# Two-layer hybrid backbone on one core: late vectors of layer 1, outputs by direction, four rounded buffers for w2, six for the dense units, decays ahead of modulation rows, ranks in four column groups

## The chip, the core and the metric

The kernel runs on one core of a Trainium2 chip. A core has five engines, each with an instruction stream of its own: TensorE (PE, with PEld for its weight loads), VectorE (DVE), ScalarE (ACT), GpSimd (POOL) and SyncE (SP), which here only issues DMAs. They meet at semaphores. The metric is the device time of one execution in microseconds (us); lower is better.

## What is computed

512 token columns (256 of context, 256 latent) go through two layers: a mixer (gated linear attention with two directions beside a short convolution), then a feed-forward part, dense in layer 0 and top-2 of 8 experts in layer 1. All is float32. The reference, cut to its skeleton:

```python
for i in range(2):                       # x: latent, xc: context, same weights
    p = split_proj(modulate(rmsnorm(x, g_mix_pre[i]), sh1, sc1) @ w_in[i])   # q k v g a_f a_b B C h
    la_f = log_sigmoid(a_f @ w_dec[0] + b_dec[0]) / 16     # a_f, a_b: 16 ranks each
    la_b = log_sigmoid(a_b @ w_dec[1] + b_dec[1]) / 16
    o = scan_forward(q, k, v, la_f) + scan_backward(q, k, v, la_b)   # chunks of 64
    y = concat(rmsnorm(o) * silu(g), B * conv3(C * h)) @ w_out[i]
    x = x + gt1 * rmsnorm(y)
    h2 = modulate(rmsnorm(x, g_ffn_pre[i]), sh2, sc2)
    x = x + gt2 * rmsnorm((silu(h2 @ w1) * (h2 @ w3)) @ w2 if i == 0 else experts(h2))
```

The shifts, scales and gates (sh1, sc1, gt1, ...) are rows of `silu(c) @ w_mod[i] + b_mod[i]`, for the latent and for the context stream.

## The kernel before

Everything is kept transposed: features on 128 partitions, the 512 tokens along the free axis, so that `x` is eight tiles of 128x512 (k = 0 to 7). Every engine has its program in one fixed order, written by hand; `plan()` fixes the order of the PSUM tiles and their banks, and with it the order in which SP loads the weights: chunks of 2 MB into four slots of `ring`, each loaded when the last reader of the slot's earlier chunk has finished. The experts then use the whole ring as 12 slots of 1 MB.

**Split products.** Projections and the dense feed-forward multiply fp32r words in three products (`product`, L755 to L757): high x high, high x low and low x high. High words are roundings. DVE makes the weights' (`split_in`, `split_unit`, `split_step`: a CAST L1683 and a subtraction L1686, of 128x1024 words for a unit). ACT makes the high words of x with the modulation (`modulate`, L1376), then the full words (L1379), and DVE subtracts for the low words (`low_row`, L1686 on `hT_rounded`). The rounded weights rotate through three buffers in the projections (`in_w_high`), three in the dense units (`w_high`) and two in the w2 steps (`w2_high`, with `ff_high` and `ff_low`).

**Start.** SP loads x and four modulation chunks. PE transposes x (L771), makes modulation rows (`mod_rows`, L719: eight fp32 products of 32 columns, in four column groups of the array), transposes them back (`mod_cols`, L727) and sums squares (L688). DVE scales x (`normalise`, L1745) and then takes all four modulation columns (`take_mods`, L1803 to L1815). ACT issues 11 small DMAs for the vectors of layer 1 (`load_vectors(1)`, the last of them w_decay, L1330), PE transposes them (`vectors(1)`, L763), and ACT takes the result before it modulates (`take_vectors(1)`, L1393).

**Mixer.** PE: q and k over the rows k; the ranks `a` as a split product with 32 output columns; DVE masks them into two copies (L1839, L1840); four products `z` with w_decay (L814) on 32 rows; v; seven rounds of scores (`scores`, L845) between the projections g, C, h and B, for whose masks DVE builds decays (`differences`, L1934) and takes the scores (L1890); modulation rows ("keys"); transposed keys `kt` (L870); chunk products `U` (L885); DVE's chain of states for both directions (L1981, L1983), and then PE's outputs `o` (L901, and L913 with the states). The convolutions `conv(0)` to `conv(3)` (L1898 to L1918) are DVE's, and conv(3) stands ahead of the decays for the states (L1944, ACT's exponential L1479, L1949). ACT copies the modulation rows (`take_rows`, L1409) ahead of those exponentials.

**Feed-forward.** Layer 0: 44 units of 24 products (gate and up), three of them started row by row; then w2 in 2 x 22 steps of 12 products. Layer 1: experts of 65 to 128 tokens take the split path `mid` (L1163 to L1170), those under 65 the path `few` (L1093, L1119), which streams 42 MB in plain fp32.

## Time and profile before

| what | value |
|---|---|
| median of 3 runs | 1905.54 us (1905.01 to 1905.95) |
| profiled execution: its time / its span | 1906.78 / 1905.0 us |
| PE busy / DVE busy / ACT busy | 89% / 49% / 28% |
| DMA queue of the weights | 474 MB, mean 250 GB/s over the span |

The span is the time from the first to the last instruction; 1.78 us of the execution lie around it. The first 945 us are the mixers and the dense part, the other 960 the experts. In a timeline row the idle time of the engine ahead of an instruction stands in brackets, with what ended it.

### The profile page before, as it was taken

The numbers are of one execution on the slowest core, as the hardware profiler recorded it, in microseconds if no ns is written. First come the engines' busy times: TensorE is split into PE (matmuls) and PEld (weight loads), VectorE is DVE, ScalarE is ACT, GpSimd is POOL, SyncE is SP. The second block draws the span as 40 slices with busy tenths as digits, with TensorE's granted clock in tenths as the row PEclk, the third lists the DMA queues.
The fourth block names the chain that finished last, engine by engine and source line by source line (L and its number), as shares of the span: only waits on it lengthen the run. The fifth ranks groups of instructions, "written<-read, shape, count | busy, mean of one in ns | idle before, by whom it ended". The sixth has DMA issues, their size and how long they took to land.

```text
span 1905.0 us, 20538 instructions
## 1 busy us (share of the span) xinstructions
PE 1700.9 (89%) x8358; PEld 1151.1 (60%) x8358; DVE 941.1 (49%) x1291; ACT 536.5 (28%) x682; POOL 5.0 (0%) x14
## 2 busy tenths in 40 slices
PE   5899899999999998989899799887877999787877
PEld 2688665888887775877688688433236873322322
DVE  3388665544436666693588688301017871010102
ACT  2521134300000015323477477100005750000001
POOL 0000000000000000000000000000000000000000
PEclk8899999999999998999799999998998999989998
DMA  9210775233221244333799699699999988999996
GB/s 358 91 57 32 261 270 186 80 116 105 88 78 45 78 172 152 118 139 131 269 375 374 220 374 376 252 394 394 394 394 381 382 325 313 396 391 394 394 394 257
DMA packets 223832, 476.26 MB, mean 250 GB/s; under 512 B 9906, under 2 KB 32724, under 8 KB 223700
## 3 DMA queue, kind: packets, MB, share of 16 engines
q1 hardware_dynamic: 222176, 474.24, 68.1%
q8 instruction: 88, 1.44, 0.3%
q10 hardware_dynamic: 1524, 0.21, 0.1%
q14 instruction: 44, 0.36, 0.1%
HBM read 473.38 MB, written 1.05 MB: 249 GB/s over the span
## 4 chain that ended last, share of the span: by engine, by line
PE 72%; DMA 11%; DVE 5%; SPq 5%; issue 4%; ACT 2%; ACTq 1%; DVEq 0%; POOL 0%; POOLq 0%
PE ps L755 11%; PE ps L756 11%; PE ps L757 11%; DMA ring<-in_e_w 10%; PE ps L1093 7%; PE ps L1163 6%; PE ps L1165 6%; PE ps L1170 6%; SPq L629 3%; PE ps L1119 2%; PE ps L688 2%; SPq L633 2%; PE ps L719 2%; PE ps L951 1%; PE ps L1050 1%
## 5 line engine op out<-in xcount | busy, mean ns | idle before, releaser
L1093 PE MATMUL ps<-ring,work 128*64 128x512 f32 x1120 | 278.3, 645 | 80.6 <-DMA ring<-in_e_w 60.7
L1093 PEld LDWEIGHTS ps<-ring,work 128*64 128x64 f32 x1120 | 90.5, 148 | 247.9 <-issue 247.9
L2158 DVE TENSOR_TENSOR mixT<-work,ps 64x256 f32<-64x256 f32 x70 | 29.7, 424 | 417.3 <-ACT work L1567 416.2
L1686 DVE TENSOR_TENSOR ring_rounded<-ring,hT_rounded 128x2048 fp32r<-128x2048 f32 x84 | 191.7, 2288 | 27.8 <-ACT hT_rounded L1586 20.5
L755 PE MATMUL ps<-ring_rounded 128*128 128x512 f32 (+2 forms) x464 | 171.5, 370 | 7.1 <-DVE hT_rounded L1686 5.2
L1586 ACT CAST hT_rounded<-ring 128x2048 fp32r<-128x2048 f32 x84 | 159.9, 1911 | 46.4 <-PE ps L1165 36.2
L757 PE MATMUL ps<-ring_rounded 128*128 128x512 f32 (+2 forms) x400 | 142.3, 356 | 0.0
L755 PE MATMUL ps<-mixT_rounded,work_rounded 128*128 128x512 f32 x352 | 137.7, 391 | 2.9 <-DVE hT_rounded L1686 2.1
L757 PE MATMUL ps<-mixT_rounded,ring_rounded 128*128 128x512 f32 x352 | 137.4, 390 | 0.0
L756 PE MATMUL ps<-hT_rounded,work_rounded 128*128 128x512 f32 x352 | 137.4, 390 | 0.0
L1119 PE MATMUL ps<-ring,mixT 128*64 128x512 f32 x560 | 125.8, 593 | 0.0
L1163 PE MATMUL ps<-hT_rounded,work_rounded 128*128 128x512 f32 x252 | 103.4, 410 | 21.7 <-issue 18.5
L756 PE MATMUL ps<-hT_rounded,ring_rounded 128*128 128x512 f32 (+2 forms) x336 | 117.8, 351 | 0.0
L1683 DVE CAST work_rounded<-ring 128x1024 fp32r<-128x1024 f32 (+1 forms) x88 | 49.1, 558 | 121.7 <-PE ps L757 121.7
L1686 DVE TENSOR_TENSOR ring_rounded<-ring,norms_rounded 128x2048 fp32r<-128x2048 f32 x42 | 96.1, 2289 | 23.1 <-ACT norms_rounded L1586 23.1
L755 PEld LDWEIGHTS ps<-ring_rounded 128*128 128x128 f32 (+1 forms) x464 | 89.1, 192 | 27.4 <-issue 10.0
L1165 PE MATMUL ps<-hT_rounded,work_rounded 128*128 128x512 f32 x252 | 101.2, 401 | 0.0
L1170 PE MATMUL ps<-ring_rounded,work_rounded 128*128 128x512 f32 x336 | 91.8, 396 | 0.0
L1119 PEld LDWEIGHTS ps<-ring,mixT 128*64 128x64 f32 x560 | 41.6, 137 | 76.1 <-issue 70.0
L1569 ACT COPY mixT<-ps 128x256 f32<-128x256 f32 x35 | 13.0, 373 | 256.7 <-PE ps L1107 256.7
L1686 DVE TENSOR_TENSOR ring_rounded<-ring,work_rounded 128x1024 fp32r<-128x1024 f32 (+1 forms) x88 | 84.1, 955 | 1.5
L757 PEld LDWEIGHTS ps<-ring_rounded 128*128 128x128 f32 (+1 forms) x400 | 75.9, 190 | 11.7
(247 smaller groups left out, 2663.5 us busy)
## 6 DMA issues: line engine op xcount, KB each, us to landing
ring<-in_e_w SPq DMA_DIRECT2D x336, 1024.0 KB, 14.1
ring<-in_w_mod SPq DMA_DIRECT2D x24, 2048.0 KB, 9.6
ring<-in_w_in SPq DMA_DIRECT2D x12, 2048.0 KB, 7.9
ring<-in_w SPq DMA_DIRECT2D x22, 1024.0 KB, 7.9
ring<-in_w_out SPq DMA_DIRECT2D x4, 2048.0 KB, 13.7
ring<-in_w SPq DMA_DIRECT2D x4, 2048.0 KB, 7.9
ring<-in_w SPq DMA_DIRECT2D x2, 1536.0 KB, 9.2
mixT<-in_ctx SPq DMA_DIRECT2D x2, 512.0 KB, 4.3
```

The source lines that it names most:

```text
L629: sp.dma_start(dst.rearrange("p (k n) -> p k n", k=4), rows(w[0, e, k0 * P:(k0 + 4) * P], b * BLK, BLK)).then_inc(piece_in[s], 16)
L755: pe.matmul(acc, w_high_, x_high_, start=first, stop=False)
L756: pe.matmul(acc, w_high_, x_low_, start=False, stop=False)
L757: return pe.matmul(acc, w_low_, x_high_, start=False, stop=last)
L1093: ins = pe.matmul(acc[H * w:H * w + H, :], x[:, k, 0:H], piece_words(e, b, 2 * half + w)[:, kk * BLK:(kk + 1) * BLK], start=(k == 0), stop ...
L1119: ins = pe.matmul(ps[0][H * half:H * half + H, :], eh[:, b % 2, ((j % 2) * 2 + j // 2) * H:][:, 0:H], piece_words(e, b, 4 + i)[:, o:o + BL ...
L1163: pe.matmul(outs[q], high[q], w_high_[:, cols], start=q < first, stop=False, skip_group_check=True)
L1165: ins = pe.matmul(outs[q], low[q], w_high_[:, cols], start=False, stop=False, skip_group_check=True)
L1170: ins = pe.matmul(outs[q], high[q], w_low_[:, q * BLK:(q + 1) * BLK], start=False, stop=q >= 4 - last, skip_group_check=True)
L1586: act.copy(highs[at_ % HIGHS], piece_words(e, b, i)).then_inc(high_ready, 1)
L1683: return dve.tensor_copy(dst, src)
L1686: return dve.tensor_tensor(dst, src, high, ALU.subtract)
```

## The change

- `vectors(1)` and its loads come after layer 0's `z`; w_decay has a semaphore of its own and is loaded four times, once for each group of 32 partitions. ACT issues these 18 small DMAs behind layer 0's modulation.
- The start: DVE takes modulation columns 0 and 1 ahead of the scaling, columns 2 and 3 after three of its eight rows, and scales the others between the splits. `modulate` waits for each half of the scale alone.
- `row_products`: in the row-by-row stages (q/k, first three dense units) PE does both products with x's high words on all tiles, then the products with the low words.
- `a` is no longer a split unit: 16 plain fp32 products in four column groups, and `z` sums over all 128 partitions.
- conv(3) comes after the "keys" modulation columns, and ACT takes these rows after the exponentials of the decays.
- Outputs by direction: `states_ready` counts directions. Layer 0 does its heads in two pairs; layer 1 does all four heads with direction 0, then the modulation rows `states1`, then direction 1.
- Six rounded buffers for the dense units, four for w2's row tiles; the first two w2 steps are split ahead of the last unit's product. The split of `qk` 3 of layer 1 stands inside `normalise`.

```diff
-    IN_UNITS += [("qk", L_, p) for p in range(PAIRS)] + [("a", L_, 0)] + [("v", L_, p) for p in range(PAIRS)]
+    IN_UNITS += [("qk", L_, p) for p in range(PAIRS)] + [("v", L_, p) for p in range(PAIRS)]
...
+        w2_parts = [part(at_, 3, 512, of=of) for of, at_ in ((ring_r, HIGH_AT), (ring_r, HIGH_AT + 1536), (work_r, 0),
+                                                             (work_r, 1536))]
+        def unit_high(u):
+            return in_w_high[:, u - 3].rearrange("p (k n) -> p k n", k=KD) if 3 <= u < 6 else w_high[:, u % 3]
...
+            def row_products(n, tiles, x_high_, x_low_, first, last):
+                pe.wait_ge(high_row, n + 1)
+                for acc, c0, w_high_, w_low_ in tiles:
+                    pe.matmul(acc, w_high_, x_high_[:, c0:], start=first, stop=False)
+                    pe.matmul(acc, w_low_, x_high_[:, c0:], start=False, stop=False)
+                pe.wait_ge(x_split, n + 1)
+                for acc, c0, w_high_, w_low_ in tiles:
+                    ins = pe.matmul(acc, w_high_, x_low_[:, c0:], start=False, stop=last)
...
             mod_cols(*start[-1])
-            vectors(1)
...
-                project_in(("a", L), ("a", L, 0), 0, width=2 * RANK)
+                for x_ in (in_high, x_low):
+                    for kk in range(2):
+                        for g in range(4):
+                            k = 4 * kk + g
+                            ins = pe.matmul(acc[2 * RANK * g:2 * RANK * (g + 1), :], w[:, k, 0:2 * RANK],
+                                            x_[:, k, :].bitcast(F32), start=(kk == 0 and x_ is in_high),
+                                            stop=(kk == 1 and x_ is x_low), skip_group_check=True)
...
+                if L == 0:
+                    vectors(1)
...
-                mods("states1" if L else "states")
+                if L == 0:
+                    mods("states")
...
+                for pairs in ((0,), (1,)) if L == 0 else ((0, 1),):
...
+                    for d in range(2):
+                        if L and d == 1:
+                            mods("states1")
+                        pe.wait_ge(states_ready, 2 * L + d + 1)
+                        pe.wait_ge(state_ops, 4 * L + 3 + d)
...
-                wait_mods(layer, s + 1)
+                    if k in (0, 4):
+                        act.wait_ge(mod_ready, 12 * layer + 2 * s + 3 + k // 4)
...
-            load_vectors(1)
-            take_vectors(1)
...
                 modulate(2 * L, L, 0, 0, in_high)
+                if L == 0:
+                    for layer in range(DEPTH):
+                        load_decay(layer)
+                    load_vectors(1)
...
-                take_rows(*MODS["keys1" if L else "keys"])
-
                 for d in range(2):
                     act.wait_ge(state_diff, 2 * L + d + 1)
...
+                take_rows(*MODS["keys1" if L else "keys"])
...
-                if k == 0:
-                    wait_tile(dve, unit_tile(UNITS - 1) if half == 0 else ("y2", 3))
+                if d in (2, 3):
+                    wait_tile(dve, unit_tile(UNITS - 1))
...
-            normalise(0, 0)
-            take_mods(*MODS["start"])
+            take_mods(*MODS["start"][0:2])
+            r = inverse(TOK)
+            for k in range(3):
+                divide(hT[:, k, :], xT[:, k, :], r)
+            take_mods(*MODS["start"][2:4])
...
-                conv(3)
...
                 take_mods(*MODS["keys1" if L else "keys"])
+                conv(3)
...
+                        if j == JF - 1:
+                            split_step(0)
+                            split_step(1)
```

What now stands where, on the engines that wait there. DVE at the start, from the scaling of x (`hT<-xT,norms`) to the first low word of x (`hT_rounded`); before:

```order
L1679 COPY xT<-ps 128x512 x8
L1745 TENSOR_TENSOR hT<-xT,norms 128x512 x8
L1803 TENSOR_REDUCE modv<-ps 128x8
L1807 TENSOR_TENSOR modv<-modv,vecs 128x8
...
L1683 CAST ring_rounded<-ring 128x1024
L1686 TENSOR_TENSOR ring_rounded<-ring,ring_rounded 128x1024
L1686 TENSOR_TENSOR hT_rounded<-hT,ring_rounded 128x512 x2
```

The same stretch now:

```order
L1738 COPY xT<-ps 128x512 x8
L1863 TENSOR_REDUCE modv<-ps 128x8
L1867 TENSOR_TENSOR modv<-modv,vecs 128x8
L1863 TENSOR_REDUCE modv<-ps 128x8
L1867 TENSOR_TENSOR modv<-modv,vecs 128x8
L1803 TENSOR_TENSOR hT<-xT,norms 128x512 x3
...
L1742 CAST ring_rounded<-ring 128x1024
L1745 TENSOR_TENSOR ring_rounded<-ring,ring_rounded 128x1024
L1745 TENSOR_TENSOR hT_rounded<-hT,ring_rounded 128x512
L1803 TENSOR_TENSOR hT<-xT,norms 128x512
```

Two modulation columns moved ahead of the scaling, and five of its eight rows behind the first split. PE from the ranks to v (`work,ring` is z, `ident,work` the vectors); before and now:

```order
L755 MATMUL ps<-ring_rounded 32x512
L756 MATMUL ps<-hT_rounded,ring_rounded 32x512
L757 MATMUL ps<-ring_rounded 32x512
L814 MATMUL ps<-work,ring 128x512 x4
L755 MATMUL ps<-ring_rounded 128x512
```

```order
L842 MATMUL ps<-ring_rounded,ring 32x512 x8
L842 MATMUL ps<-hT_rounded,ring 32x512 x8
L851 MATMUL ps<-work,ring 128x512 x4
L793 MATMUL ps<-ident,work 128x113
L770 MATMUL ps<-ring_rounded 128x512
```

Eight such triples became 16 plain products, and the vectors stand behind z. DVE at the end of layer 0's scores, from the last taken level but one; before and now:

```order
L1890 COPY_PREDICATED work<-masks,ps 128x512 x4
L1898 TENSOR_TENSOR norms<-norms,ps 128x512
...
L1918 TENSOR_TENSOR mixT<-mixT,ps 128x512
L1944 TENSOR_TENSOR work<-work 128x1024 x2
L1949 TENSOR_TENSOR work<-work 128x1024 x2
```

```order
L1955 COPY_PREDICATED work<-masks,ps 128x512 x4
L2008 TENSOR_TENSOR work<-work 128x1024 x2
L2013 TENSOR_TENSOR work<-work 128x1024 x2
L1955 COPY_PREDICATED work<-masks,ps 128x512 x4
L2017 TENSOR_TENSOR work<-work 128x1024 x2
```

The six instructions of conv(3) left the stretch ahead of the decays.

## Rows read from the trace of the kernel before

**Rows 1.** Waits of PE: by whom, total, times, longest.
```profile
PE ps L1093 <- DMA ring<-in_e_w: 60.7, 25, 3.5
```
**Rows 2.** Waits of SP's DMA queue for a slot.
```profile
SPq L629 <- PE ps L1170: 252.1, 84, 21.9
```
**Rows 3.** Timeline, the start.
```profile
31.82 1.92 PE L719 MATMUL ps<-ring,csil 128*32 128x512 f32 x16 [0.55 <-DMA ring<-in_w_mod]
32.80 4.91 DVE L1745 TENSOR_TENSOR hT<-xT,norms 128x512 f32<-128x512 f32 x8 [14.49 <-ACT norms L1361]
37.86 1.11 PE L727 MATMUL ps<-ident,ring 128*128 128x128 f32 x4 [4.11 <-DVE modv L1803]
47.84 0.45 PE L763 MATMUL ps<-ident,work 113*128 113x113 f32 x1 [6.96 <-DMA ring<-in_w_decay]
51.41 0.76 PE L755 MATMUL ps<-ring_rounded 128*128 128x512 f32 x1 [3.13 <-DVE hT_rounded L1686]
```
**Rows 4.** DMA issues of 18.9 to 19.3 (q/k) and 243.3 to 243.6 (w_out): KB, us to landing.
```profile
ring<-in_w_in SPq DMA_DIRECT2D x1, 2048.0 KB, 18.9
ring<-in_w_out SPq DMA_DIRECT2D x1, 2048.0 KB, 13.4
```
**Rows 5.** Stretches: length, PE busy (instructions), PEclk, DMA share, GB/s.
```profile
81.30:113.40 32.10, 30.61 (x107) 0.84 0.23 85
82.80:89.10 6.30, 6.30 (x9) 0.57 0.93 338
352.25:575.50 223.25, 223.25 (x984) 1.00 0.29 92
732.20:739.00 6.80, 6.00 (x20) 0.50 0.68 260
758.50:788.90 30.40, 28.91 (x107) 0.89 0.25 90
```
**Rows 6.** Timeline, z in layers 0 and 1.
```profile
82.79 6.33 PE L814 MATMUL ps<-work,ring 32*128 32x512 f32 x8 [1.49 <-DVE work L1840]
760.04 4.35 PE L814 MATMUL ps<-work,ring 32*128 32x512 f32 x8 [1.49 <-DVE work L1840]
```
**Rows 7.** Timeline, layer 0 from the scores to y.
```profile
224.67 3.65 PE L870 MATMUL ps<-ident,work 128*128 128x128 f32 x16 [3.37 <-DVE work L1890]
246.15 2.02 PE L901 MATMUL ps<-work 128*128 128x128 f32 x16 [0.77 <-DVE small L1992]
256.78 0.69 DVE L1683 CAST ring_rounded<-ring 128x1024 fp32r<-128x1024 f32 x1 [5.83 <-DMA ring<-in_w_out]
257.51 1.23 DVE L1686 TENSOR_TENSOR ring_rounded<-ring,ring_rounded 128x1024 fp32r<-128x1024 f32 x1
269.28 0.50 PE L755 MATMUL ps<-ring_rounded 128*128 128x512 f32 x1 [0.78 <-DVE norms L2008]
```
**Rows 8.** Timeline, dense part and entry of layer 1.
```profile
330.55 1.09 ACT L1376 ACTIVATE mixT_rounded<-hT,modv 128x256 fp32r<-128x256 f32 x2
352.25 0.47 PE L755 MATMUL ps<-mixT_rounded,work_rounded 128*128 128x512 f32 x1 [0.85 <-DVE ring_rounded L1686]
578.28 0.47 PE L755 MATMUL ps<-work_rounded 128*128 128x512 f32 x1 [2.75 <-DVE ring_rounded L1686]
642.14 0.47 PE L755 MATMUL ps<-work_rounded 128*128 128x512 f32 x1 [2.15 <-DVE ring_rounded L1686]
733.00 0.55 PE L755 MATMUL ps<-ring_rounded 128*128 128x256 f32 x1 [2.07 <-DVE hT_rounded L1686]
```
**Rows 9.** Timeline, layer 1 from the scores to y.
```profile
854.11 2.76 PE L870 MATMUL ps<-ident,work 128*128 128x128 f32 x16 [2.63 <-DVE work L1949]
859.36 3.81 DVE L1983 SCALAR_TENSOR_TENSOR hT<-hT,dec,ps 128x128 f32<-128x128 f32 x12
865.22 3.57 PE L719 MATMUL ps<-ring,csil 128*32 128x512 f32 x16 [3.03 <-DVE hT L1983]
878.95 1.32 PE L951 MATMUL ps<-mixT,ring 128*128 128x256 f32 x5 [0.56 <-issue]
```

More of the change, by code:

```diff
@@ L376, in hybrid_backbone @@
         iota_t = work[:, 1408:1408 + TOK].bitcast(I32)
[L377 removed]
+        iota_r = work[:, 1920:1921].bitcast(I32)
         itmp = work[:, 2048:2048 + P]
@@ L748, in project_in @@
                 for k in range(KD):
-                    ins = product(acc[0:width, 0:TOK - c0], high[:, k, :], low[:, k, :], in_high[:, k, c0:],
+                    ins = product(acc[:, 0:TOK - c0], high[:, k, :], low[:, k, :], in_high[:, k, c0:],
                                   x_low[:, k, c0:], k == 0, k == KD - 1)
@@ L799, in _ @@
                         high, low = in_unit(("qk", L, k // 2))
[L800 to L806 removed]
+                    tiles = [(accs[i][:, 0:TOK - job[3]], job[3], high[:, k % 2, i * P:(i + 1) * P],
+                              low[:, k % 2, i * P:(i + 1) * P]) for i, job in enumerate(jobs)]
+                    ins = row_products(2 * L * KD + k, tiles, in_high[:, k, :], x_low[:, k, :], k == 0, k == KD - 1)
                     if k % 2 and k < KD - 1:
                         ins.then_inc(pair_used, 1)
[L809 removed]
+                acc = begin(("a", L))
+                w = weights(("a", L))
+                for x_ in (in_high, x_low):
[5 more added lines that the diff above has]
+                                            stop=(kk == 1 and x_ is x_low), skip_group_check=True)
+                end(ins)
                 wait_drained(pe, ("a", L))
+                pe.wait_ge(wdec_in, 16 * 4 * DEPTH)
                 for i in range(4):
@@ L971, in _ @@
                         pe.wait_ge(w_split, u + 1)
-                        high, low = w_high[:, u % 3], unit_weights(u, ring_r)
+                        high, low = unit_high(u), unit_weights(u, ring_r)
                         for k in range(KD):
@@ L1676, in _ @@
             dve.tensor_copy(itmp, ident[:]).then_inc(consts_done, 1)
+            band = rank_rows[:, 1:2]
+            step(dve.tensor_scalar(band, iota_r, -0.5, None, ALU.is_gt))
+            for edge in range(RANK, P, RANK):
+                wait_step()
+                step(dve.scalar_tensor_tensor(out=band, in0=iota_r, scalar=edge - 0.5, in1=band, op0=ALU.is_gt,
+                                              op1=ALU.subtract))
+            wait_step()
+            step(dve.tensor_scalar(rank_rows[:, 0:1], band, -1.0, None, ALU.mult))
+            step(dve.tensor_scalar(band, band, 1.0, None, ALU.add))
             for k in range(KD):
@@ L1751, in inverse, with normalise @@
                 return rs[:, (n_rs[0] - 1) % 2, 0:n]
-            def normalise(norm, c0, split=None):
+            def normalise(norm, c0, split=None, between=()):
                 r = inverse(TOK - c0)
@@ L1759, in normalise @@
                         low_row(norm, k - 2, *split)
+                    if k == 5:
+                        split_in(*between)
                 if split:
@@ L2039, in _ @@
                                ("ffu", j))
-                    for d in range(2 * JF):
+                    for d in range(2, 2 * JF):
                         split_step(d)
+                    wait_step_used(dve, 2 * JF - 3)
                     split_in(("qk", 1, 0), ("qk", 1, 1), ("qk", 1, 2))
```

134 lines of the change are left out of this document (67 added, 67 removed).

## The prediction

> **What bounds the kernel now.** First the page, for whether there is one bound: PE is busy 89% of the span (the table above), yet it isn't the bound everywhere. PE's waits, by whom, show the difference: in the sparse experts (L1093) it waits 60.7 us for expert weights [rows 1], and there the DMA stream sets the pace. SP's own waits show the reverse for the split experts: its queue waits 252.1 us, 84 times, for PE's L1170 to give a slot back [rows 2]. Two of the three split experts come first (945 to 1217 us). So the stream is ahead of PE when the sparse ones begin, and an earlier start of the experts moves everything behind it by as much. What is left are the first 945 us. All edits lie there, and I read them as a timeline, gap by gap: at each I ask who ends PE's wait, and who would end it next. The instants below are those of the trace of before.
>
> **The start.** Three things in a row hold PE until 51.41 [rows 3]: DVE's scaling (from 32.80, 4.91 us) stands ahead of the modulation columns, so PE waits 4.11 us until 37.86; then the vectors of layer 1 cost a DMA round trip (6.96 us of idle before 47.84); then comes the first low row. What doesn't move is the DMA queue: the fourth modulation chunk ends PE's wait at 31.82 [rows 3], and q/k's chunk, issued at 19.01, lands 18.9 us later, at 37.9 [rows 4]. Afterwards: modulation rows until 33.8, columns and copy with 0.8 us between them until 36.4; ACT modulates from 35.3. DVE can split q/k's first unit only at 37.9: 0.69 + 1.23 us [rows 7], with the handover 2.0, so PE starts at **40.0**. From there PE wants 12 products of 0.227 us a row (223.25 us for 984 products [rows 5]), 2.7 us; ACT needs 1.97 (four instructions; a pair takes 1.09 [rows 8]), DVE 2.3 (half a split, a scaling of 0.62, a low row of 0.69). PE stays the bound. Gain 11.4. The clock is low when PE starts, as before; I put the same loss in both, and 1.5 us either way in the range. The 18 DMA issues on ACT take some 0.32 us each, 5.8 us behind the last modulated row, until 58.3; q's drain behind them is due at 64, w_decay at 67, so they are hidden. Without that cover they would cost up to 5.8.
>
> **Ranks, z and v.** Before, in layer 0, `a` takes 24 products of 0.231 = 5.55 us. Now 16 plain fp32 products in four column groups: the modulation rows do eight such in 1.92 us with four groups [rows 3], so 3.6. DVE's masks stay (1.49 us [rows 6]). z took 6.33 and 4.35 us [rows 6], and in layer 0 the granted clock was 0.57 while PE was busy without a break [rows 5]: ahead of the fall PE had run 32-column products, then 32-row ones. z at 2.4 GHz is 8 records of 0.43 = 3.5 (a quarter of 1.92 us is a round of four groups, 0.48 at most). Nearest row for the clock: the modulation rows at 31.8, at full clock, the same pattern. I take the full clock; v then needs 96 x 0.227 = 21.8 us. Layer 0: from the end of q/k, 37.6 us (5.55 for `a` and 32.10 up to the scores [rows 5]) become 0.1 + 3.6 + 1.5 + 3.5 + 0.4 (vectors) + 21.8 = 30.9, gain **6.7**. Layer 1: 35.9 (5.5 and 30.4 [rows 5]) become 31.0, gain **4.9**; in this, 0.6 us is a new wait, since DVE reaches the masks late, behind its splits of v. If the clock stays as it was, both gains shrink by 4 (kept for the range).
> The Trainium skill's page "TensorE: Matmul & The Clock Gate", section "Measured speedup vs the span model", gives three column groups only 2.38 times the speed; by that share (0.79) `a` would take 4.6 us, and the sum would be 2 us smaller. The row speaks for nearly full overlap: 8 products of 0.43 x 2 in 1.92 us.
>
> **Layer 0, scores to y.** PE waits 3.37 us ahead of kt, which then runs at the low clock (3.65 us) [rows 7]. conv(3) and ACT's copies of modulation rows stood ahead of the exponentials; with both moved, DVE is done by 212 and kt can start at 221.3. With 2.0 us for kt, no 0.43 wait behind it and no wait for the states (0.77 [rows 7]), PE's outputs end at 249.8 instead of 256.7, 6.8 us earlier. But another chain ends last: DVE waits 5.83 us for w_out [rows 7], issued at 243.4 and landed 13.4 us later [rows 4], behind a queue that moves 2 MB in 5.4 us. Its chunks are back to back from 213 on; only the late ones lose a gap, so w_out lands at 255.1, not 256.8. Three unit splits (5.8) and the columns "outputs" follow, which free the banks for the sums of squares: these start at 261.7 and not 264.6, y at 266.3 instead of 269.28. Gain **3.0**; 6.8 would be the other end. Moved conv(3) holds banks: h's is read by 222.9, B's by 226.3, and PE wants them at 227.0. Hidden by 0.7 us.
>
> **Dense part.** Entry: the first high row is there at 331.6, PE started at 333.49 on the low row. PE then also ends the three units earlier, and unit 3, whose buffer no longer waits, is split by 349.6 (DVE free at 347.6). Unit 3 starts at 349.9 instead of 352.25 [rows 8]: **2.3**. Entry of w2: 2.75 us of wait [rows 8] goes, and with it a stretch at half clock of 3.4 us, worth 1.7. Middle of w2: 2.15 [rows 8] and again 1.7. Together **8.2** (4.9 if the clock falls nonetheless). Steps 2 and 3 wait for the last unit, but the first two steps give them 5.4 us, and they need 2.7. The last buffers now delay the splits of q/k 1 on DVE until 5.4 us before PE's end there; they take 5.8, and DVE isn't wanted before PE's sums are done 3.5 us later.
>
> **Entry of layer 1.** PE waits 2.07 us for the low row [rows 8]; the high row is there some 1.9 earlier. 732.2 to 739.0 ran at half clock [rows 5]. If it holds, PE is paced by ACT (1.97 a row) and ends 5.5 earlier; if not, 1.9. I take **4.0**, as the gap ahead shrinks to 0.2 us but PE has only short work around it.
>
> **Layer 1, scores to y.** DVE is busy without a break from 790 to 847 and sets the pace; it starts when v ends, so that stretch only shifts. Behind it: kt waits 2.63 us, `states1` waits 3.03 for a bank that DVE's states hold and runs at the low clock (3.57 against 1.92), o waits behind it [rows 9]. Now: the decays are ready at 848.7, columns end at 851.7, kt and U end at 858.4; conv(3) lets DVE start the states at 854.6, direction 0 is done 4.6 us later (3.81 of it the chain [rows 9]) at 859.2, where the last bank frees. Attention 2.1, direction 0 2.0, modulation rows 1.9 and column 1.4 cover direction 1 (863.8), outputs end at 868.6 instead of 876.0, y starts at 871.6 against 878.95 [rows 9]: **7.4**.
>
> **Sum.** 11.4 + 6.7 + 3.0 + 2.3 + 8.2 + 4.0 + 4.9 + 7.4 = 47.9 us. From the span of 1905.0: 1857.1, with 1.78 around it 1858.9 for that execution, whose time is 1.2 above the median. From the median: 1905.54 - 47.9 = **1857.6 us**.
>
> **Rivals.**
> (a) The clock isn't held: z and v stay slow (-8), entry of layer 1 gives 1.9 (-2.1), w2 keeps its two half-clock stretches (-3.3). 1871. For it: the low clock followed each of these gaps. Against: the gaps go.
> (b) Column groups don't overlap: 32 records of 0.43 = 13.8 us in each layer, 20.4 more: 1878. Against: L719's row.
> (c) More comes back: w_out doesn't hold y (+3.8) and the entry of layer 1 gives 5.5 (+1.5), first rows at full clock (+2): 1850. For it: the clock ran full over gaps of 0.8 us.
> (d) The edits don't reach the end, because expert weights bound the split experts too: 1905. Against: [rows 2]; the first expert DMA is released by y's products.
> (e) Slower: the four-group ranks leave PE at 1.2 GHz through layer 0's scores (113.4 to 215.7, PE busy throughout). Half clock makes 102 us 204, 102 more than before against 47.9 gained: 1960; it turns slower once 48 us of work at full clock run at half. For it: z did run slow while PE was busy [rows 5]. Against: v woke the clock within 11 us.
>
> **Chances.** Forecast (1852 to 1866) 0.60; (a) 0.16; (c) 0.12; (b) 0.05; (d) 0.03; (e) 0.02; 0.02 for new waits that eat the rest. The range 1848 to 1874 holds forecast, (a) and (c). 0.2% (3.8 us) is about what a measurement of this kernel can tell from no change: faster 0.95, same 0.03, slower 0.02.
>
> **What would show it.** First split product near 40 with DVE's first split released by q/k's DMA; `a` at 3.6 us and z at 3.5 with PEclk 1.00; DVE's wait for w_out growing to about 10 us; no PE gap at w2's entry or middle; kt without a wait in both layers; `states1` between two groups of L913's kind; expert rows unchanged in length. I am wrong if PE waits for ACT's or DVE's rows between 40 and 65, if the clock rows around z stay below 1, or if waits for expert DMA appear before 1170.

## The result, and the profile after

The changed kernel takes 1859.10 us, the median of four runs (1858.12 to 1859.89), against 1905.28 (1904.92 to 1905.95) for the kernel before on the same chip: 46.2 us less, a ratio of 0.9757 with a 95% interval of 0.9746 to 0.9768. The forecast was 1857.6, in a range of 1848 to 1874. The profiled execution spans 1857.3 us, 47.7 less than before.

The page of the kernel after, its first parts. In part 2 each digit is a fortieth of the span, in tenths.

```profile
span 1857.3 us, 20588 instructions
PE 1677.3 (90%) x8374; PEld 1136.0 (61%) x8374; DVE 940.2 (51%) x1297; ACT 535.8 (29%) x682; POOL 5.0 (0%) x14
PEclk9999999999999999998899999998989999899898
```

The waits of PE in the kernel after, the costliest: by whom, us in total, times, longest.

```profile
PE ps L1133 <- DMA ring<-in_e_w: 59.0, 24, 3.5
...
PE ps L703 <- DVE modv L1863: 5.1, 1, 5.1
```

The first row answers [rows 1]: 60.7 us before, 59.0 now. The sparse experts wait for their weights as before, so the stream didn't eat the gain. The second row is new, and it is the place where the forecast was wrong.

**The start.** The timeline of PE and DVE in the kernel after: start, duration, engine, line, operation, and in brackets the idle time ahead of it with what ended it. It answers [rows 3].

```profile
39.92 0.76 PE L780 MATMUL ps<-ring_rounded 128*128 128x512 f32 x1 [4.50 <-ACT ring_rounded L1422]
...
37.72 0.69 DVE L1742 CAST ring_rounded<-ring 128x1024 fp32r<-128x1024 f32 x1 [1.59 <-DMA ring<-in_w_in]
38.45 1.23 DVE L1745 TENSOR_TENSOR ring_rounded<-ring,ring_rounded 128x1024 fp32r<-128x1024 f32 x1
```

The first split product moved from 51.41 to 39.92. The trace names ACT as what ended PE's wait, but ACT's first row of high words (L1422, from 34.71) was written by 35.8, and DVE's split ends at 39.7. The split is what came last (the repetition e12 names it, with a wait of 3.68 us), and it waited for q/k's chunk. This is the floor that the prediction named.

**Ranks and z.** Timeline of PE in the kernel after, both layers, for [rows 6]. The two rows of L842 are the rank product in four column groups.

```profile
63.58 1.92 PE L842 MATMUL ps<-ring_rounded,ring 128*32 128x512 f32 x16
65.32 1.90 PE L842 MATMUL ps<-hT_rounded,ring 128*32 128x512 f32 x16
68.75 3.70 PE L851 MATMUL ps<-work,ring 128*128 128x512 f32 x8 [1.53 <-DVE work L1905]
...
722.01 3.70 PE L851 MATMUL ps<-work,ring 128*128 128x512 f32 x8 [1.53 <-DVE work L1905]
```

z takes 3.70 us in both layers, where it took 6.33 and 4.35. The rank product takes 3.6 us from the start of its first record (63.58) to the end of its last (67.22).

**Layer 0, ahead of y.** DVE's and PE's timeline in the kernel after, for [rows 7].

```profile
237.07 0.69 DVE L1742 CAST ring_rounded<-ring 128x1024 fp32r<-128x1024 f32 x1 [11.53 <-DMA ring<-in_w_out]
...
242.67 0.18 DVE L1863 TENSOR_REDUCE modv<-ps 128x8 f32<-128x32 f32 x1
...
237.68 0.63 PE L742 MATMUL ps<-ident,ring 128*128 128x128 f32 x4 [0.82 <-ACT ring L1456]
243.41 6.05 PE L703 MATMUL ps<-norms,ones 128*128 128x512 f32 x8 [5.10 <-DVE modv L1863]
249.90 0.50 PE L770 MATMUL ps<-ring_rounded 128*128 128x512 f32 x1 [0.44 <-DVE norms L2073]
```

PE is done with the modulation columns at 238.3 and waits 5.10 us. DVE, which stands 11.53 us in front of w_out, has three unit splits to do before it reads those columns and so frees the banks. The sums of squares behind the wait take 6.05 us, most of them at the low clock (see below), where they took 3.89 in the kernel before.

**Dense part and layer 1.** Timeline of PE in the kernel after, for [rows 8] and [rows 9]: unit 3, first row of layer 1, k transposed, `states1`, y.

```profile
330.29 0.47 PE L770 MATMUL ps<-mixT_rounded,ring_rounded 128*128 128x512 f32 x1 [0.96 <-DVE ring_rounded L1745]
...
699.06 0.35 PE L780 MATMUL ps<-ring_rounded 128*128 128x256 f32 x1 [0.36 <-ACT ring_rounded L1422]
...
810.75 1.91 PE L909 MATMUL ps<-ident,work 128*128 128x128 f32 x16
...
818.47 2.02 PE L940 MATMUL ps<-work 128*128 128x128 f32 x16 [1.29 <-DVE small L2042]
...
822.35 1.92 PE L734 MATMUL ps<-ring,csil 128*32 128x512 f32 x16
...
830.54 0.67 PE L995 MATMUL ps<-mixT,ring 128*128 128x256 f32 x2 [0.55 <-issue]
```

From 330.29 to 677.10, where w2 ends, PE has no gap above 0.1 us: the two waits ahead of and within w2 (2.75 and 2.15 us in [rows 8]) are gone. In layer 1 kt starts without its wait of 2.63, and `states1` runs in 1.92 us where it took 3.57 behind a wait of 3.03. A smaller wait of 1.29 stands ahead of the outputs now.

**The clock.** Stretches of the kernel after: length, then busy us and instructions of PE, PEld, DVE, ACT and POOL, granted clock, DMA share, GB/s.

```profile
36.56:43.39 6.83, 3.46 (x8) 2.81 (x9) 5.60 (x8) 6.64 (x15) 0.00 (x0) 0.50 1.05 387
72.32:94.36 22.04, 22.04 (x100) 17.99 (x98) 14.85 (x15) 8.61 (x11) 0.00 (x0) 1.00 0.18 67
...
241.36:248.19 6.83, 4.78 (x6) 1.99 (x7) 2.50 (x10) 1.50 (x3) 0.00 (x0) 0.50 1.09 359
```

A clock of 0.50 is 1.2 GHz, 1.00 is 2.4. Before 872 us it is at 0.50 twice: at the first products (from 36.56) and in the new wait and at the sums of squares behind it (from 241.36). The falls in z, at kt, at the dense entry, around w2 and in layer 1 up to y have gone, and in this trace the one at the sums of the second residual too.

### The profile page after: what moved, and what is told of

It reads as the page before. It is cut to its first block, busy times and chain, and to the rows that moved or that the text cites. A ratio compares the mean times of both kernels' runs of the same rounds, so it can differ in the third digit from the quotient of the medians.

```text
span 1857.3 us, 20588 instructions
## 1 busy us (share of the span) xinstructions
PE 1677.3 (90%) x8374; PEld 1136.0 (61%) x8374; DVE 940.2 (51%) x1297; ACT 535.8 (29%) x682; POOL 5.0 (0%) x14
## 4 chain that ended last, share of the span: by engine, by line
PE 68%; DMA 13%; SPq 6%; issue 4%; DVE 4%; ACT 3%; ACTq 0%; DVEq 0%
DMA ring<-in_e_w 11%; PE ps L770 9%; PE ps L771 9%; PE ps L772 9%; PE ps L1133 7%; PE ps L1203 6%; PE ps L1205 6%; PE ps L1210 6%; SPq L644 3%; SPq L648 2%; PE ps L1159 2%; DMA ring<-in_w_mod 2%; PE ps L703 2%; PE ps L995 2%; PE ps L1090 1%
## 5 line engine op out<-in xcount | busy, mean ns | idle before, releaser
L770 PE MATMUL ps<-ring_rounded 128*128 128x512 f32 (+1 forms) x472 | 171.9, 364 | 1.5 <-DVE ring_rounded L1745 1.1
L772 PE MATMUL ps<-ring_rounded 128*128 128x512 f32 (+1 forms) x408 | 145.2, 356 | 0.0
L772 PE MATMUL ps<-mixT_rounded,ring_rounded 128*128 128x512 f32 x328 | 127.6, 389 | 0.0
L1203 PE MATMUL ps<-hT_rounded,work_rounded 128*128 128x512 f32 x252 | 103.5, 411 | 21.7 <-issue 18.4
L770 PE MATMUL ps<-mixT_rounded,work_rounded 128*128 128x512 f32 x304 | 118.3, 389 | 0.0
L771 PE MATMUL ps<-hT_rounded,work_rounded 128*128 128x512 f32 x304 | 118.3, 389 | 0.0
L1745 DVE TENSOR_TENSOR ring_rounded<-ring,norms_rounded 128x2048 fp32r<-128x2048 f32 x42 | 96.1, 2289 | 23.1 <-ACT norms_rounded L1636 23.1
L1205 PE MATMUL ps<-hT_rounded,work_rounded 128*128 128x512 f32 x252 | 101.2, 402 | 0.0
L770 PEld LDWEIGHTS ps<-ring_rounded 128*128 128x128 f32 x472 | 89.1, 189 | 17.6 <-issue 2.0
L771 PE MATMUL ps<-hT_rounded,ring_rounded 128*128 128x512 f32 (+1 forms) x280 | 95.4, 341 | 0.0
L1742 DVE CAST work_rounded<-ring 128x1024 fp32r<-128x1024 f32 (+1 forms) x63 | 37.7, 598 | 113.2 <-PE ps L772 113.2
L1745 DVE TENSOR_TENSOR ring_rounded<-ring,ring_rounded 128x1024 fp32r<-128x1024 f32 (+1 forms) x81 | 87.4, 1079 | 2.0
L772 PEld LDWEIGHTS ps<-ring_rounded 128*128 128x128 f32 x408 | 77.1, 189 | 11.0
```

The source lines that it names most:

```text
L770: pe.matmul(acc, w_high_, x_high_, start=first, stop=False)
L771: pe.matmul(acc, w_high_, x_low_, start=False, stop=False)
L772: return pe.matmul(acc, w_low_, x_high_, start=False, stop=last)
L1203: pe.matmul(outs[q], high[q], w_high_[:, cols], start=q < first, stop=False, skip_group_check=True)
L1205: ins = pe.matmul(outs[q], low[q], w_high_[:, cols], start=False, stop=False, skip_group_check=True)
L1742: return dve.tensor_copy(dst, src)
```

## The experiments

Twelve kernels ran: eleven edits of the kernel after (e10 and e11 build on e1's) and, in the last group, the kernel after itself again (e12), to show how far two sets of runs differ. The groups ran on different chips. Not undone by themselves are the six buffers of the dense units and the split of `qk` 3 inside `normalise`. Each time is the median of 4 or 5 runs. Executions of one kernel lie up to 7 us apart (e2), so a step is read from its instants in the trace first, and from the median second. The last column is by how much PE's timeline, set against that of the kernel after, shifts across the place named.

| kernel | what is undone or changed | median, us (range) | ratio to before, 95% | shift of PE's timeline there, us |
|---|---|---|---|---|
| e12 | nothing | 1858.04 (1856.94 to 1858.92) | 0.9739 to 0.9765 | start -1.1 |
| e8 | vectors of layer 1 early again | 1860.87 (1860.14 to 1861.47) | 0.9755 to 0.9789 | start +4.1 |
| e9 | columns behind the whole normalised input | 1862.49 (1859.12 to 1863.99) | 0.9755 to 0.9785 | start +2.1, then +3.1 |
| e7 | products wait for the low row | 1861.63 (1861.04 to 1863.86) | 0.9759 to 0.9795 | start 0, dense +3.0, layer 1 +1.5 |
| e2 | old ranks | 1868.91 (1863.80 to 1871.20) | 0.9782 to 0.9827 | layer 0 +4.0, layer 1 +5.4 |
| e3 | old ranks, z from 128 rows | 1862.04 (1858.42 to 1864.83) | 0.9749 to 0.9786 | +2.1 and +2.0 |
| e4 | two buffers for w2 | 1867.04 (1864.63 to 1868.05) | 0.9777 to 0.9809 | +8.5 |
| e5 | conv(3) and rows ahead of the decays | 1863.37 (1860.93 to 1864.96) | 0.9761 to 0.9798 | layer 0 -1.4, layer 1 +5.4 |
| e6 | outputs wait for both directions | 1859.98 (1857.99 to 1861.09) | 0.9745 to 0.9780 | layer 0 -0.9, layer 1 +1.7 |
| e1 | w_out's first chunk early | 1854.96 (1852.94 to 1858.82) | 0.9723 to 0.9756 | start +1.7, y -5.0 |
| e10 | e1, with e5's edit in layer 0 | 1856.77 (1856.14 to 1857.95) | 0.9733 to 0.9763 | y -1.1 |
| e11 | w_out's chunks swapped, (1,0) behind y | 1861.13 (1858.17 to 1864.24) | 0.9756 to 0.9783 | y -4.4, behind y +8.1 |

**The missed term: w_out early (e1).** The edit moves one transfer in SP's order.

```diff
     chunk_order.insert(chunk_order.index(("mod", *MODS["residual"][0])), ("ff", 0))
+    chunk_order.remove(("wo", 0, 0))
+    chunk_order.insert(chunk_order.index(("mod", 1, 0)), ("wo", 0, 0))
```

> The kernel after (1859.1 us), with w_out's first chunk of layer 0 asked for ahead of modulation chunk (1,0) instead of behind it. In the kernel after, VectorE waits 11.5 us for that chunk (it lands at 237.05), the modulation columns it hands on at 243.4 make TensorE wait 5.1 us, its next products run at a granted clock of 0.5 (6.05 us instead of 3.89), and layer 0's y starts at 249.90. Theory, w_out's transfer holds y: it lands one chunk earlier, at about 231.8, TensorE's wait of 5.1 us goes or shrinks below 1, the clock stays at 1.0 through the sums, y starts at about 245.9, and the kernel takes about 1855. Rival, the chain of TensorE's own products holds y: 1859, y at 249.9. A third: modulation chunk (1,0), now later, is what is waited for (it landed at 231.8 and would land at 237): the wait stays and the time is 1859 or above.

DVE's and PE's timeline with w_out early:

```profile
232.65 0.69 DVE L1744 CAST ring_rounded<-ring 128x1024 fp32r<-128x1024 f32 x1 [5.39 <-DMA ring<-in_w_out]
...
238.16 1.92 PE L736 MATMUL ps<-ring,csil 128*32 128x512 f32 x16 [2.23 <-DMA ring<-in_w_mod]
...
241.99 3.89 PE L705 MATMUL ps<-norms,ones 128*128 128x512 f32 x8
246.65 0.50 PE L772 MATMUL ps<-ring_rounded 128*128 128x512 f32 x1 [0.77 <-DVE norms L2075]
```

The first theory holds. The chunk is split at 232.65 instead of 237.07, PE's wait of 5.1 becomes one of 2.2 for chunk (1,0), the sums run at 3.89 us, and y starts at 246.65. This execution was 1.7 us behind at 214 (0.4 at its first product, 1.3 because the products behind it ran longer at the low clock), so the stage itself gained 5.0 us. The median is 4.1 us below 1859.1, and 3.1 below the repetition's 1858.0. The intervals of the ratios still overlap by a little (0.9723 to 0.9756 against 0.9739 to 0.9765). In the trace y is clearly earlier, and the medians point the same way; that the whole kernel gains these 5.0 us isn't shown. Of the 6.2 us by which this span is shorter than that of the kernel after, 1.7 are there at layer 1's y (1.5 were lost at the second residual's sums, where the clock fell), and 4.5 come in the router's stage and the experts, which the edit doesn't touch.

**Is w_out the only cover? (e10)** In the same kernel the convolution and ACT's rows are put back ahead of the decays, in layer 0 alone; DVE's part of the edit:

```diff
+                if L == 0:
+                    conv(3)
                 wait_tile(dve, ("P", L, len(LEVELS) - 1, 3))
...
-                conv(3)
+                if L:
+                    conv(3)
```

> The kernel with w_out's first chunk early (y of layer 0 at 246.65, 1855.0), with the convolution of the fourth key tile and ScalarE's modulation rows back ahead of the decays in layer 0 alone. Behind w_out's late chunk this move was worth nothing in layer 0 (y at 249.42 with it undone, 249.90 without). Theory, w_out was the only cover: now TensorE's wait of 3.4 us before k transposed and the slow products behind it reach y, which starts at 250 to 252: +3.5 to +5, about 1859. Rival, another wait covers it as well (modulation chunk (1,0), 2.2 us of wait in the kernel with w_out early): +1 to +2.

PE's timeline of that kernel:

```profile
205.42 3.65 PE L911 MATMUL ps<-ident,work 128*128 128x128 f32 x16 [3.36 <-DVE work L1960]
...
248.61 0.50 PE L772 MATMUL ps<-ring_rounded 128*128 128x512 f32 x1 [0.77 <-DVE norms L2081]
```

Against e1, each read from where it stood ahead of kt, y comes 3.9 us later (1.1 gained on the kernel after, where e1 gains 5.0). The expectation was 3.5 to 5. Of the 6.0 us that PE loses at kt (3.36 of wait, 1.7 of slower products, and what follows), 2.1 went into the wait for chunk (1,0). So both theories have a part: w_out was the main cover, and that chunk covers a third. The medians differ by 1.8 only, with ranges that overlap.

**The same edit with w_out late (e5).** The kernel after with conv(3) and ACT's rows back ahead of the decays in both layers.

> The kernel after, with VectorE's convolution of the fourth key tile, and ScalarE's modulation rows, in their old places around the decays in both layers. Theory: in layer 1 nothing else holds this stretch, TensorE's old wait of 2.63 us before k transposed comes back with a low clock behind it, about +3.5; in layer 0 w_out's transfer, which lands at 237.05 whatever TensorE does, takes the lost 3 us in, 0 to +0.4: 1863. Rival, layer 0 pays in full as well: 1866.

PE's timeline, layer 0 and layer 1:

```profile
206.55 3.30 PE L909 MATMUL ps<-ident,work 128*128 128x128 f32 x16 [3.37 <-DVE work L1955]
...
244.75 3.89 PE L703 MATMUL ps<-norms,ones 128*128 128x512 f32 x8
249.42 0.50 PE L770 MATMUL ps<-ring_rounded 128*128 128x512 f32 x1 [0.77 <-DVE norms L2073]
...
814.92 3.68 PE L909 MATMUL ps<-ident,work 128*128 128x128 f32 x16 [2.63 <-DVE work L2014]
```

In layer 0, PE falls 5.7 us further behind the kernel after up to its outputs, and y still starts at 249.42 instead of 249.90. The reordering is worth nothing there, even a little less: PE arrives at the sums without a wait and does them in 3.89 us, not in 6.05 behind a wait. In layer 1 the timeline loses 5.4 us, more than the 3.5 expected: 2.63 of wait, and 1.8 at kt and 0.8 in U, which run at the low clock (813.52 to 820.35). The rival (layer 0 pays in full) is out. That the median met the expected 1863 is partly luck: layer 1 paid 1.9 more than expected and layer 0 gained 1.4.

**Outputs by direction (e6).** The waits for direction 0 and 1 are put together again, and `states1` ahead of them.

```diff
-                        if L and d == 1:
-                            mods("states1")
-                        pe.wait_ge(states_ready, 2 * L + d + 1)
-                        pe.wait_ge(state_ops, 4 * L + 3 + d)
...
```

> The kernel after, with the outputs waiting for both directions' states again in both layers, and layer 1's modulation products ahead of them. Theory: layer 1 pays TensorE's wait of 3.03 us and part of a low clock, now 1.29 us of it is there: +2 to +3.5; layer 0 pays nothing, because w_out's transfer takes the wait in: 1862. Rival, layer 0 pays 0.8 to 3 as well: above 1863.5.

PE's timeline of that kernel at `states1`:

```profile
822.19 1.92 PE L734 MATMUL ps<-ring,csil 128*32 128x512 f32 x16 [3.07 <-DVE hT L2045]
```

The old wait of 3.03 is back (3.07), but the clock didn't fall behind it (1.92 us for the rows). Less the 1.29 that it replaces, layer 1 pays 1.7 us, a little below the expected 2 to 3.5. In layer 0 a wait of 1 us ahead of the outputs was taken in by w_out, as expected.

**The ranks: which shape lowers the clock? (e2, e3)** e2 brings the split unit, its 24 products and the masks on 32 rows back. e3 does the same but masks all 128 rows, zero above 32, so that only z's shape differs from e2.

```diff
-                for x_ in (in_high, x_low):
-                    for kk in range(2):
-                        for g in range(4):
...
+                project_in(("a", L), ("a", L, 0), 0, width=2 * RANK)
```

> The kernel after, with the rank product of both layers back in its old form: a split unit of 32 columns for each of the 8 row tiles, 24 products, and z from 32 rows. Theory of the prediction, the narrow shapes themselves lower the clock: the granted clock is 0.5 to 0.6 for some microseconds around a and z (as at 82.8 to 89.1 and 732.2 to 739.0 of the kernel before), z takes 6.3 in layer 0 and 4.4 in layer 1, and the two layers together lose about 12 us: 1871. Rival, only the time of the products counts and the clock stays where it is now: 1.9 us for a in each layer and a split of some 0.7: about 1864.

> The rank product in its old form as in the kernel with old ranks, but z still from 128 rows, those above 32 set to zero by the mask. It parts the two shapes that the change altered. If z's 32 rows are what lowers the clock: clock 1.0 in z (3.70 us), about +4 us, all of it a's own time: 1863. If the 32 columns of a do it: as the kernel with old ranks, about 1871.

z in e2, and stretches of e2, then of e3:

```profile
71.49 3.70 PE L844 MATMUL ps<-work,ring 32*128 32x512 f32 x8 [1.49 <-DVE work L1898]
728.40 5.24 PE L844 MATMUL ps<-work,ring 32*128 32x512 f32 x8 [1.49 <-DVE work L1898]
```

```profile
75.05:78.47 3.42, 3.42 (x10) 2.67 (x10) 0.00 (x0) 3.21 (x7) 0.00 (x0) 0.50 0.62 230
...
730.41:737.24 6.83, 6.83 (x13) 3.57 (x12) 0.00 (x0) 4.90 (x8) 0.00 (x0) 0.50 0.55 207
```

```profile
74.50:96.60 22.10, 22.10 (x100) 18.06 (x99) 14.85 (x15) 8.64 (x13) 0.00 (x0) 1.00 0.10 37
729.70:751.70 22.00, 22.00 (x99) 17.92 (x97) 13.79 (x15) 8.50 (x11) 0.00 (x0) 1.00 0.10 37
```

With z on 32 rows the clock falls at z's end in layer 0 (z itself took 3.70 us, not the 6.3 expected) and inside z in layer 1, with PE busy throughout the stretch. With z on 128 rows, the same 24 narrow products of 32 columns and the same wait (1.50 us) ahead of it, it doesn't. Nor does it in any other kernel here with 128 rows. So `a`'s 32 columns alone don't lower the clock, and z's 32 rows are needed for it. Whether they do it without `a`'s narrow products ahead isn't shown: no kernel has z on 32 rows behind the new rank product. Of e2's 9.4 us in the trace, 4.1 is the rank product's own time (e3) and 5.3 the clock, by the end of v. The forecast had put 4 us a layer on the clock; it is 1.9 in layer 0 and 3.4 in layer 1.

**Two buffers for w2 (e4).**

```diff
-                if d >= 4:
-                    wait_step_used(dve, d - 4)
+                if k >= 2:
+                    dve.wait_ge(w2_used, half * (JF - 1) + k - 1)
...
-                    for d in range(2, 2 * JF):
+                    for d in range(2 * JF):
```

> The kernel after, with two buffers for w2's row tiles again and the two waits that go with them (the first two row tiles are not split ahead of the last unit's gate, and the second half's first split waits for the first half's end). Theory of the prediction: the two gaps of 2.75 and 2.15 us come back and the clock falls to 0.5 for 3.4 us behind each, as at 578.3 and 642.1 of the kernel before: 4.9 + 3.5 = 8.4 us, 1867.5. Rival, only the waits count: 4.9, 1864.0.

Its timeline of PE, and its stretches behind the two waits:

```profile
556.98 0.76 PE L770 MATMUL ps<-work_rounded 128*128 128x512 f32 x1 [2.75 <-DVE ring_rounded L1745]
620.67 0.47 PE L770 MATMUL ps<-work_rounded 128*128 128x512 f32 x1 [2.15 <-DVE ring_rounded L1745]
```

```profile
556.58:559.99 3.41, 3.01 (x7) 2.46 (x8) 2.12 (x5) 0.00 (x0) 0.00 (x0) 0.50 0.00 0
621.43:624.85 3.42, 3.42 (x10) 2.65 (x9) 0.96 (x2) 0.00 (x0) 0.00 (x0) 0.50 0.00 0
```

Both waits return to the hundredth, each with its 3.4 us at half clock. The timeline loses 8.5 us, 8.4 expected.

**The start, in parts (e8, e9).** e8 loads, transposes and takes the vectors of layer 1 at the start. e9 has DVE normalise all eight tiles ahead of all modulation columns.

```diff
-            r = inverse(TOK)
-            for k in range(3):
-                divide(hT[:, k, :], xT[:, k, :], r)
-            take_mods(*MODS["start"][2:4])
+            normalise(0, 0)
+            take_mods(*MODS["start"])
```

> The kernel after, with layer 1's vectors loaded, transposed and taken at the start of the program again. Theory: the transposes and their answers stand ahead of TensorE's first split product (39.92) and of the normalised input on VectorE: +5 to +6 us, all of it still there at the end: 1864.6. Rival, the start waits for the q/k chunk (released at about 38) anyway and part is hidden: +1 to +2.

> The kernel after, with VectorE's normalised input whole ahead of all four chunks' modulation columns again, as before the change; the low parts first and the late vectors stay. The first split product is at 39.92 in the kernel after, where q/k's chunk and ScalarE's first modulated row end together. Theory: the columns come 4.9 - 1.9 = 3 to 4 us later, ScalarE's rows with them, and the start goes to about 43.6: +3.7 at the end, 1862.8. Rival: with the vectors out of the way there is room until q/k's chunk lands, and the first product moves by less than 1.5 us.

PE's timeline in e8, then in e9:

```profile
42.18 0.45 PE L792 MATMUL ps<-ident,work 113*128 113x113 f32 x1 [6.87 <-DMA work<-in_conv_w]
44.05 0.77 PE L779 MATMUL ps<-ring_rounded 128*128 128x512 f32 x1 [1.42 <-ACT ring_rounded L1420]
```

```profile
36.65 0.66 PE L742 MATMUL ps<-ident,ring 128*128 128x128 f32 x4 [3.47 <-DVE modv L1863]
...
42.04 0.77 PE L780 MATMUL ps<-ring_rounded 128*128 128x512 f32 x1 [2.82 <-DVE ring_rounded L1745]
```

Undone alone, the vectors cost 4.1 us at the start and 3.9 at y, a little less than expected. The median rose by 1.8 only (1864.6 was expected), so not all of it is still there at the end: the trace is 3.8 us behind at layer 1's y and 1.4 at the first expert, since its router's stage, which the edit doesn't touch, ran 2.4 us faster. Undone alone, the columns cost 2.1 us at the first product and 3.1 by the end of its stage, between the two theories: q/k's chunk hides some of it. The median met the theory's 1862.8, but with 2.5 us from two falls of the clock far behind the edit (689.32 and 798.55). Both and the low row together were worth 11.5. The parts don't add up; that each was a wait behind the other, so that the chunk hides part of one alone, fits the traces, but the two were not undone together.

**The low row (e7).** The products of a row again wait for its low part.

```diff
-                    pe.matmul(acc, w_high_, x_high_[:, c0:], start=first, stop=False)
-                    pe.matmul(acc, w_low_, x_high_[:, c0:], start=False, stop=False)
...
+                    ins = product(acc, w_high_, w_low_, x_high_[:, c0:], x_low_[:, c0:], first, last)
```

> The kernel after, with the products of the first units of the dense feed-forward and of each layer's entry waiting for a row's low part before any product of the row, as before the change. Theory of the prediction: gaps of 0.3 to 0.9 us a row come back in the second to eighth rows where VectorE is behind: about 1 us in the dense part, 4 in layer 1's entry with a low clock, 0.8 at the start: 1865. Rival, the gaps are there but the clock holds: 1862.

PE's timeline at the entry of the dense part and of layer 1, and the stretch at low clock:

```profile
313.12 0.77 PE L770 MATMUL ps<-mixT_rounded,work_rounded 128*128 128x512 f32 x1 [2.07 <-DVE hT_rounded L1742]
...
702.77 0.36 PE L770 MATMUL ps<-ring_rounded 128*128 128x256 f32 x1 [2.07 <-DVE hT_rounded L1742]
```

```profile
312.37:319.19 6.82, 6.07 (x14) 4.79 (x15) 4.80 (x8) 6.82 (x15) 0.00 (x0) 0.50 0.89 282
```

The wait of 2.07 us returns at both places, against 0.36 in the kernel after. The expectation had the split wrong: the dense part pays 3.0 (1 expected), since the clock fell there; layer 1 pays 1.5 (4 expected), since it didn't; of the 0.8 expected at the start nothing shows. The sum of 4.5 lies between rival and theory.

**Chunk (1,0) behind y (e11).**

```diff
-        "states": ((0, 8), (0, 9)), "outputs": ((0, 10), (0, 11), (1, 0)), "residual": ((1, 1), (1, 2)),
+        "states": ((0, 8), (0, 9)), "outputs": ((0, 10), (0, 11)), "residual": ((1, 0), (1, 1), (1, 2)),
...
+    chunk_order.remove(("wo", 0, 0))
+    chunk_order.insert(chunk_order.index(("ff", 0)), ("wo", 0, 0))
```

> The kernel with w_out's first chunk early, and modulation chunk (1,0) multiplied among the residual's chunks behind y instead of among those ahead of it. Theory: the wait of 2.2 us for that chunk goes, and with it 2.6 us of rows and column ahead of y; the sums start when VectorE has split w_out and read the columns (about 238.9), y starts at 243.5 instead of 246.65, and 2.6 us of this come back behind y, where TensorE has no gap: 0.5 below the kernel with w_out early, 1854.5. Rival: the residual's first rows wait for the chunk, or y for VectorE, and it is slower than that kernel by 1 to 2.

DVE's and PE's timeline of that kernel, ahead of y and behind it:

```profile
237.68 0.69 DVE L1744 CAST ring_rounded<-ring 128x1024 fp32r<-128x1024 f32 x1 [11.35 <-DMA ring<-in_w_out]
...
243.51 3.78 PE L705 MATMUL ps<-norms,ones 128*128 128x512 f32 x4 [5.22 <-DVE modv L1865]
246.30 1.42 PE L772 MATMUL ps<-ring_rounded 128*128 128x512 f32 x1
...
300.02 3.10 PE L736 MATMUL ps<-ring,csil 128*32 128x512 f32 x16 [2.15 <-DMA ring<-in_w_mod]
```

The kernel doesn't do what its expectation says. The edit put w_out's first chunk behind its second, so DVE got it at 237.68 again. y is early all the same (four of the eight sums ran ahead of the wait), but 8.1 us are lost after its start: 1.8 in y's first products, which run at the low clock, 2.6 for the rows and the column of (1,0), 2.15 of wait for a chunk, and 1.6 of low clock behind that. What the move of (1,0) is worth beside an early w_out stays open. As it stands it is slower than e1.

**The kernel after again (e12).**

> The kernel after, unchanged, on the same chip as the three others of this group, so that the version with w_out early and (1,0) behind y is compared with it side by side. 1859.1 was measured; every theory says the same again, within 2. The clock falls once more at the sums of squares of layer 0 (0.5 at about 241 to 248), and whether it also falls at the sums of the second residual (7.67 us there before, 9.0 to 9.3 in four of the kernels tried) is open.

It took 1858.04 us. Its traced execution starts its first product 1.1 us earlier (38.83) and is 1.4 ahead at 870. The wait of 5.10 is 4.70 here and the sums take 6.21, so the term that the forecast missed repeats. The clock falls at the sums of layer 0 once more (240.17 to 247.0) and not at those of the second residual.

## Why the prediction was right, and where it wasn't

The time each step gave is the difference of the same instants in the traces of before and after.

| step | forecast | measured | instants, before to after |
|---|---|---|---|
| start | 11.4 | 11.5 | first split product, 51.41 to 39.92 |
| ranks, z, v of layer 0 | 6.7 | 7.5 | end of v, 113.32 to 94.29 |
| layer 0, scores to y | 3.0 | 0.35 | y, 269.28 to 249.90 |
| dense entry | 2.3 | 2.6 | unit 3, 352.25 to 330.29 |
| w2 | 8.2 | 8.65 | its end, 707.72 to 677.10 |
| sums of the second residual | none | 1.6 | 9.27 long, now 7.67 |
| entry of layer 1 | 4.0 | 3.9 | wait 2.07 to 0.36 (1.7), rows 2.2 |
| ranks, z, v of layer 1 | 4.9 | 5.3 | end of v, 788.84 to 747.44 |
| layer 1, scores to y | 7.4 | 7.0 | y, 878.95 to 830.54 |
| sum at y | 47.9 | 48.4 | |

Behind y, 1.2 us are given back in the router's stage, where the clock is at 0.50 for 18.1 us and was for 14.2, and 0.5 come again in the experts; the span ends 47.7 earlier.

**The start** was right in its size and in what ends last: q/k's chunk. e8 and e9 show that the two large parts are real, and that neither has its full value alone.

**The step that failed is the sum for layer 0, scores to y**, 3.0 against 0.35. The mechanism was named (w_out's transfer, not PE, holds y, and DVE's wait for it grows), and e1, e5 and e10 confirm it. Two terms were mis-sized. The landing was forecast 1.7 us earlier than before in its own time; measured at 237.05 and set back by the 19.0 that the stages ahead had gained, it is 256.05, so 0.7 earlier. And the price of PE's new idle time was left out: PE gets there early, waits 5.1 us, and its sums take 6.05 us, most of it at 1.2 GHz, and not the 3.9 that the sum had for them, 2.15 us more (0.3 of it come back in the wait ahead of y, 0.44 for 0.78). The prediction did say that an earlier PE would wait; it didn't ask what a longer wait does to the work behind it. For layer 0 the moved convolution was worth nothing (e5), and its whole value in this kernel is in layer 1, 5.4 us.

**Ranks and z** came out at the row that the forecast had chosen. The trace shows 16 products in four column groups in 3.6 us, as [rows 3]' eight in 1.92 had it. The Trainium skill's page "TensorE: Matmul & The Clock Gate", section "Measured speedup vs the span model", measures 2.38 times for three groups of 32 columns; by my estimate from its share of the ideal this product would have taken 4.6 us, and the trace doesn't agree. The clock held, as assumed, and e2 against e3 shows what it hung on: z's rows, not `a`'s columns alone. The prediction had named both as suspects in its account of [rows 5] and didn't part them.

**w2** was right in both halves, wait and clock (e4: 8.5 when undone). **The low row** was right in sum. e7 shows that its parts depend on whether the clock falls behind the wait, which varies from place to place.

**Layer 1 from scores to y** was right at 7.0 against 7.4, though two small waits that the forecast hadn't got appeared, 0.65 for chunk (1,8) and 1.29 ahead of the outputs. When undone one by one, its parts give 5.4 (e5) and 1.7 (e6), 7.1 together.

The errors were of both signs and nearly cancelled: -2.65 at layer 0's y, +1.6 at the sums of the second residual, +1.5 in the rest. The 1.6 are luck: no part of the change aims at them, and the clock fell at the same place in five of the edited kernels. That the total came within 1.5 us of the median doesn't show that each term was right. Of these 1.5 us, 1.2 is that the execution traced of before was that much above its median. **The rivals** are settled: (a), since the clock held at z, at w2 and at the entry; (b), by 3.6 us for the rank product; (d), since the first sparse expert starts 47.2 us earlier (1217.0 before, 1169.8 now), with its waits as they were; (e), since the clock was 1.00 from 43.39 to 241.36, the scores of layer 0 in it. (c) fails too: w_out did hold y, the entry of layer 1 gave 3.9 and not 5.5, and the first products ran at the low clock until 43.39. What it hoped for at y was there to be had, 5.0 us, but it took another edit to get it (e1).

## What to carry to other kernels

Before an engine's chain is shortened, find the transfer that ends last at the same meeting point. If it is a queued load, the shortening can be worth nothing until the load moves as well, and here one transfer moved in the order of loads gave more (5.0 us in the trace) than the reordering of two engines (none in that layer). Price a new wait twice, once for itself and once for the products behind it, if the trace shows the clock falling behind waits of that length. And take a gain apart by undoing one part at a time from the final kernel: parts that stood in series hide one another.

## What the runs showed of the hardware

- The granted clock can fall while PE is busy without a break. z from 32 rows, behind 24 products of 32 columns, did it in both layers of e2 (3.42 and 6.83 us at 0.50) and of the kernel before ([rows 5]); z from 128 rows with the same number of products did it in none of the other twelve traces.
- Whether it falls behind a wait of about 1 to 3 us differs between places and between executions with the same work. A wait of 3.03 us ahead of `states1` had it in the kernel before (3.57 us for the rows), one of 3.07 at the same place in e6 didn't (1.92). At the sums of the second residual, the same 16 products behind gaps of the same kind (1.35 and 0.82) took 7.67 us in the kernel after, and 8.8 to 9.3 in e1, e4, e5, e6 and e9. In e9 the clock was at 0.50 from 798.55 to 801.96 with PE busy in all of it, where no other kernel had it. Such a fall was worth 1.1 to 1.7 us here. The first products' stretch ends between 42.2 and 48.5 in the traces of the kernel after and its edits; e1's, which ends at 46.5, cost it 1.3 us against the kernel after.

Stretches of e1 (sums of the second residual), then of e9, for this point:

```profile
684.81:688.23 3.42, 3.42 (x5) 1.30 (x4) 3.42 (x7) 0.87 (x3) 0.00 (x0) 0.50 1.03 392
```

```profile
798.55:801.96 3.41, 3.41 (x19) 3.41 (x18) 3.34 (x5) 0.00 (x0) 0.00 (x0) 0.50 0.00 0
```

- The router's stage, the same work in all (872.14 to 897.78 in the kernel after), takes 23.1 to 25.8 us, and its time at 0.50 goes with it: 10.2 to 11.5 us of it where it takes 23.1 to 23.3, 14.2 to 14.4 where it takes 24.4 to 24.7, 18.0 to 18.1 where it takes 25.6 to 25.8. So up to 2.7 us of a difference between two traces can stand in a stage that no edit touched. That this makes the spread between executions of one kernel is likely, but no run shows it.
- Four column groups overlap nearly in full: eight products of 32 columns take 1.90 to 1.92 us, where each of their records lasts 0.59 us, two for each product.
